# A hybrid decoder layer on one core: the last mixer tile gets its own order, output weights are split one tile sooner, the first output projection stands in its waits

## What is computed

```python
hn = rms_norm(x, norm_mix_g[l])
proj = hn @ w_in[l]
att = swa_sink_attention(q_a, k_a, v_a, ...)
qk_m = causal_conv_silu(jnp.concatenate([q_m, k_m], axis=-1), conv_w[l], conv_b[l])
h_m = mlstm_chunkwise(...)          # state C, n, m carried from chunk to chunk
h_m = rms_norm(h_m, ...).reshape(B, S, ML_WIDTH) * jax.nn.sigmoid(o_m)
x = x + jnp.concatenate([att, h_m], axis=-1) @ w_out[l]
x = x + hier_moe(rms_norm(x, norm_ffn_g[l]), ...)
```

## Time and profile before

| | us |
|---|---|
| median of 3 runs | 953.25 (952.66 to 955.26) |
| the profiled execution, its own time | 951.49 |
| its span from first to last instruction | 949.7 |
| TensorE busy | 875.6 (92%) |
| TensorE weight loads | 704.1 (74%) |
| VectorE busy | 617.7 (65%) |
| ScalarE busy | 563.7 (59%) |
| GpSimd busy | 250.1 (26%) |
| mean granted TensorE clock | 0.956 |

### The profile page before, as it was taken

How to read it: one execution, slowest core, us unless ns; L and a number is a source line. 1 busy time by engine, 2 the same in 40 slices (tenths; PEclk the granted TensorE clock), 3 DMA queues, 4 the chain that set the end, 5 groups by cost and what they waited for, 6 DMA issues and landing times.

```text
span 949.7 us, 18047 instructions
## 1 busy us (share of the span) xinstructions
PE 875.6 (92%) x5337; PEld 704.1 (74%) x5338; DVE 617.7 (65%) x1262; ACT 563.7 (59%) x1003; POOL 250.1 (26%) x395
## 2 busy tenths in 40 slices
PE   6799999999999976799993699999999999999994
PEld 4688888898988865578882567776768688777873
DVE  3766666656666658243467767665569699876992
ACT  3474755637374656022224368865769799787991
POOL 4101011010101100000005035544344444554442
PEclk9989999999999995899996699999999999999998
DMA  9800010101000050343447477975879799888973
GB/s 330 238 24 23 24 45 0 44 0 44 22 22 22 1 200 23 111 153 137 153 162 287 164 259 270 325 273 125 311 254 382 261 380 394 301 302 298 389 274 67
DMA packets 57646, 168.41 MB, mean 177 GB/s; under 512 B 12584, under 2 KB 14928, under 8 KB 57616
## 3 DMA queue, kind: packets, MB, share of 16 engines
q1 hardware_dynamic: 50384, 143.13, 40.6%
q0 software_dynamic: 7232, 24.92, 10.1%
HBM read 143.49 MB, written 24.54 MB: 177 GB/s over the span
## 4 chain that ended last, share of the span: by engine, by line
PE 44%; issue 27%; POOL 13%; DVE 5%; POOLq 5%; DMA 4%; ACT 2%; SPq 0%; ACTq 0%; DVEq 0%
PE bank_j L995 8%; PE bank_j L997 7%; PE bank_j L996 7%; PE bank_j L1089 5%; POOL tick L595 5%; PE bank_j L1100 3%; PE bank_o L1080 3%; POOL hn L629 2%; POOLq L640 2%; PE bank_t L989 2%; POOL out_dram L634 2%; DMA PT<-in_w_in_dram 2%; PE bank_t L1073 2%; POOL row_s L641 1%; PE bank_s L1065 1%
## 5 line engine op out<-in xcount | busy, mean ns | idle before, releaser
L995 PE MATMUL bank_j<-w_high,rows_high 128*128 128x512 f32 x512 | 208.2, 407 | 7.4 <-DVE w_low L1557 5.0
L997 PE MATMUL bank_j<-w_high,rows_low 128*128 128x512 f32 x512 | 202.6, 396 | 0.0
L996 PE MATMUL bank_j<-w_low,rows_high 128*128 128x512 f32 x512 | 202.2, 395 | 0.0
L595 POOL TENSOR_TENSOR tick<-mhalf 1x1 f32<-1x1 f32 x176 | 89.4, 514 | 200.4 <-DVE lg L1931 72.0
L995 PEld LDWEIGHTS bank_j<-w_high,rows_high 128*128 128x128 f32 x512 | 97.7, 191 | 39.4 <-issue 12.7
L1816 DVE TENSOR_TENSOR w_low<-w_res,w_high 128x1024 fp32r<-128x1024 f32 x96 | 114.2, 1218 | 7.0 <-ACT w_high L693 7.0
L997 PEld LDWEIGHTS bank_j<-w_high,rows_low 128*128 128x128 f32 x512 | 97.6, 191 | 21.2
L996 PEld LDWEIGHTS bank_j<-w_low,rows_high 128*128 128x128 f32 x512 | 98.0, 191 | 18.7
L693 ACT ACTIVATE w_high<-w_res 128x1024 fp32r<-128x1024 f32 x96 | 97.6, 1050 | 0.9 <-PE bank_j L997 0.9
L989 PE MATMUL bank_t<-ident,hn 128*128 128x128 f32 x336 | 46.4, 284 | 16.5 <-DVE hn L1587 8.5
L1089 PE MATMUL bank_j<-hnT,w_res 128*128 128x128 f32 x512 | 60.3, 277 | 0.0
(11 more groups left out here) (364 smaller groups left out, 1820.1 us busy)
## 6 DMA issues: line engine op xcount, KB each, us to landing
w_res<-in_w_gate_dram SPq DMA_DIRECT2D x48, 512.0 KB, 7.8
w_res<-in_w_up_dram SPq DMA_DIRECT2D x48, 512.0 KB, 7.2
bias<-in_w_down_dram SPq DMA_DIRECT2D x32, 512.0 KB, 7.9
slot_b<-in_w_gate_dram SPq DMA_DIRECT2D x16, 512.0 KB, 10.2
PT<-in_w_up_dram SPq DMA_DIRECT2D x16, 512.0 KB, 11.2
gmix<-in_w_down_dram SPq DMA_DIRECT2D x16, 512.0 KB, 6.7
h<-in_w_down_dram SPq DMA_DIRECT2D x16, 512.0 KB, 8.3
hn<-in_x_dram SPq DMA_DIRECT2D x8, 512.0 KB, 3.3
```

Of the source, the lines that this page charges most:

```text
L595: pool.tensor_tensor(tick[:, len(ticks):len(ticks) + 1], mhalf[0:1, 0:1], mhalf[0:1, 0:1], ALU.mult)
L995: pe.matmul(out_, ah, bh, start=start, stop=False)
L996: pe.matmul(out_, ah, bl, start=False, stop=False)
L997: return pe.matmul(out_, al, bh, start=False, stop=stop)
```

## The change

- **Output weights sooner.** In tile 6 SyncE loads tile 0's mixed rows and piece 0 of `w_out` (now into `gmix`) as soon as the buffers are free, and pieces 1 to 6 into `wres` right after the last convolution (`pe_cin`). ScalarE copies pieces 0 to 5 and VectorE subtracts 0 to 3 in tile 6; the rest is done in the last tile.
- **The last tile has a function of its own on each engine,** `last_tile` on ScalarE and VectorE, a block in `body` on TensorE. The logits come before the gates' sums, the first exponentials before the gates' exponentials, the gate rows after the first transposed probabilities.
- **The first output projection** goes by pieces (`first_out`): each piece's rows are multiplied into both banks before the next piece. Pieces 0 to 2 stand after the first scores, 3 after the second, 4 after the first values, 5 to 7 at the end.
- **The second tile's mixed rows** are loaded at the start of the last tile, transposed and split at its end; both first x tiles are loaded after the second logits.
- **Dropped:** update of the state, of the running maximum and of the weighted keys in the last tile.
- Code that both kinds of tile use is moved word for word into named functions (`keys_and_gates`, `gate_sums`, `decay_args`, `state_rows` and so on); the diff leaves these out.

```diff
-        slot_out = [*pieces_of(wres, 6), gmix[:, :], wres[:, 0:PW]]
+        slot_out = [gmix[:, :], *pieces_of(wres, 6), gmix[:, :]]
...
-                if main and not nxt:
+                if main and nxt and not ahead:
                     sp.wait_ge(pe_hnT, TILES)
                     load_mix(0)
 
+                    sp.wait_ge(dve_hn, TILES)
+                    load_out(0)
                     sp.wait_ge(pe_cin, TILES)
-                    sp.wait_ge(dve_hn, TILES)
-                    for i in range(OUTP):
-                        if i == OUTP - 1:
-                            sp.wait_ge(lo0, PIECES + 1)
+                    for i in range(1, OUTP - 1):
                         load_out(i)
+                    sp.wait_ge(lo0, PIECES + 1)
+                    load_out(OUTP - 1)
+                if main and not nxt:
+                    load_mix(1)
+                    sp.wait_ge(dve_L1, TILES)
+                    for i in range(2):
+                        sp.dma_start(xin[:, i, :], x2[i * P:(i + 1) * P, :]).then_inc(LDX[i], 16)
+                    sp.wait_ge(lo0, PIECES + OUTP)
+                    sp.dma_start(gffn[:, :], norm_ffn_g[0, :].partition_broadcast(P)).then_inc(ld_gf, 16)
...
-            sp.wait_ge(dve_L1, TILES)
-            sp.dma_start(xin[:, 0, :], x2[0:P, :]).then_inc(LDX[0], 16)
-            sp.wait_ge(lo0, PIECES + OUTP)
-            sp.dma_start(gffn[:, :], norm_ffn_g[0, :].partition_broadcast(P)).then_inc(ld_gf, 16)
...
-                act.wait_ge(pe_om, TILES)
+                act.wait_ge(pe_q if i < FC else pe_vm, TILES)
...
+            def last_tile(t, u):
+
+                act.wait_ge(pe_qkT, t + 1)
+                act.wait_ge(pe_s1, t)
+                cp(qT[:, :, :].rearrange("p a b -> p (a b)"), S0[:, :]).then_inc(act_qT, 1)
+                mix_high(0, 0)
+                act.wait_ge(act_kvg, t + 1)
+                act.wait_ge(pe_o, t)
+                cp(vw[:, u, :], kvg[:, KVW:2 * KVW]).then_inc(act_v, 1)
+                log_gates(t)
+                act.activation(warm[:, 0:1], warm[:, 1:2], ACT.Exp)
+                exps(t, 0, dve_nm0, act_p0)
+                gate_exps(t)
+                pT_copy(t, pe_pT0, act_pT0)
+                for i in range(6, OUTP):
+                    out_high(i)
+                exps(t, 1, dve_nm1, act_p1)
+                decay_exps(t)
+                pT_copy(t, pe_pT1, act_pT1)
+                mix_high(1, 1)
+                state_squares(t, t + 1)
...
+                    if into_last:
+                        out_high(0)
...
                     cp(cin[:, :, TAPS - 1:], J0[:, :].rearrange("p (a b) -> p a b", a=CC)).then_inc(act_cin, 1)
+                    if into_last:
+                        out_high(1)
...
+                    state_squares(t, t + 2)
+                if into_last:
+                    for i in range(2, 4):
+                        out_high(i)
                 if nxt:
                     act.wait_ge(pe_vm, t + 2)
                     wait(act, pe_u, t + 1)
                     cp(vm[:, :, 0:DV], J1[:, :].rearrange("p (a b) -> p a b", a=MH)).then_inc(act_vm, 1)
+                if into_last:
+                    for i in range(4, 6):
+                        out_high(i)
                 if ahead and main:
...
+            def first_out(ks):
+
+                for k in ks:
+                    pe.wait_ge(lo0, PIECES + k + 1)
+                    for half, b in enumerate((J0, J1)):
+                        if k == 0:
+                            pe.wait_ge((act_om, act_vm)[half], TILES)
+                            pe.wait_ge(dve_mixT, 2)
+                        cols = slice(half * HALF, (half + 1) * HALF)
+                        ins = three(b[:, :], MX[0][0][:, k, :], MX[0][1][:, k, :], wo_h[:, k, cols], wo_l[:, k, cols],
+                                    k == 0, k == KC - 1)
+                        if k == KC - 1:
+                            ins.then_inc((pe_y0, pe_y1)[half], 1)
...
+                if main and not nxt:
+                    pe.wait_ge(act_qT, t + 1)
+                    pe.wait_ge(dve_kg, t + 1)
+                    scores(0, pe_s0)
+                    k_rows()
+                    first_out(range(0, 3))
+                    pe.wait_ge(dve_L0, t + 1)
+                    scores(1, pe_s1)
+                    first_out([3])
+                    pe.wait_ge(act_p0, t + 1)
+                    probs_T(pe_pT0)
+                    pe.wait_ge(act_pT0, t + 1)
+                    pe.wait_ge(dve_pT0, t + 1)
+                    gate_rows()
+                    pe.wait_ge(act_v, t + 1)
+                    pe.wait_ge(dve_att, t)
+                    values(0, pe_pv0)
+                    first_out([4])
+                    pe.wait_ge(dve_darg, t + 1)
+                    pe.wait_ge(dve_qg, t + 1)
+                    pe.wait_ge(act_p1, t + 1)
+                    probs_T(pe_pT1)
+                    state_scores()
+                    pe.wait_ge(act_pT1, t + 1)
+                    pe.wait_ge(dve_pT1, t + 1)
+                    values(1, pe_o)
+                    state_values()
+                    mix_T(1)
+                    first_out(range(5, OUTP))
+                    return
...
-            pe.wait_ge(dve_mix, TILES)
-            pe.wait_ge(dve_C, TILES)
+            pe.wait_ge(dve_gT, TILES)
...
+            def last_tile(t, u):
+
+                keys_and_gates(t, u)
+                mix_low(0, 0)
+                dve.wait_ge(pe_pT1, t)
+                logits(t, 0, pe_s0, dve_L0, dve_nm0)
+                gate_sums(t)
+                out_low(4)
+                pT_copy(t, pe_pT0, dve_pT0)
+                logits(t, 1, pe_s1, dve_L1, dve_nm1)
+                decay_args(t)
+                out_low(5)
+                pT_copy(t, pe_pT1, dve_pT1)
+                state_weights(t)
+                for i in range(6, OUTP):
+                    out_low(i)
+                attention(t)
+                state_scales(t)
+                add_first_half(0, 0)
+                mix_low(1, 1)
+                state_rows(t)
...
+                    if into_last:
+                        out_low(0)
...
+                if into_last:
+                    for i in range(1, 4):
+                        out_low(i)
...
+                if first:
+                    dve.wait_ge(ld_gf, 16)
+                    chain(dve.tensor_scalar(gffn[:, :], gffn[:, :], float(D) ** 0.5, None, ALU.mult))
+                    dve.wait_ge(st_mix, 16 * TILES)
```

More of the change, by code:

```diff
@@ L488, in body2 @@
             def body2(t, u, first, last):
-                if not last:
+                if not first and not last:
                     load_mix(t + 1)
@@ L738, in body @@
             def body(t, u, main, nxt, ahead):
                 v = 1 - u
+                if main and not nxt:
+                    last_tile(t, u)
+                    return
+                into_last = main and not ahead
                 if ahead and not main and not nxt:
@@ L762, in body @@
                     cp(vw[:, u, :], kvg[:, KVW:2 * KVW]).then_inc(act_v, 1)
-                    act.wait_ge(dve_az, t + 1)
-                    chain(act.activation(gfz[32:32 + MH, 1, :], gfz[32:32 + MH, 0, :], ACT.Exp, scale=-1.0))
-                    act.activation(gfz[32:32 + MH, 1, :], gfz[32:32 + MH, 1, :], ACT.Ln, bias=1.0).then_inc(act_ln, 1)
-                    if not nxt:
-                        for i in range(4):
-                            out_high(i)
+                    log_gates(t)
                 if nxt:
@@ L1022, in project_out @@
                     pe.wait_ge(dve_mixT, 2 * t + 2)
[L1023 to L1026 removed]
+                pe.wait_ge(read, t)
                 cols = slice(half * HALF, (half + 1) * HALF)
@@ new lines, in state_rows @@
+            def state_rows(t):
+                dve.wait_ge(pool_rhm, t + 1)
+                dve.wait_ge(act_om, t + 1)
+                chain(dve.tensor_tensor(hrr[:, :], hden[:, :], hrs[:, :], ALU.mult))
+                for h in range(MH):
+                    c = h // 2
+                    ins = dve.scalar_tensor_tensor(
+                        mix[:, AW + h * DV:AW + (h + 1) * DV], (S0, S1)[h % 2][:, c * VE:c * VE + DV],
+                        hrr[:, h:h + 1], osg[:, h * DV:(h + 1) * DV], ALU.mult, ALU.mult)
+                ins.then_inc(dve_mix, 1)
@@ L1590, in body @@
             def body(t, u, main, nxt, ahead):
-                v = 1 - u
+                if main and not nxt:
+                    last_tile(t, u)
+                    return
+                into_last = main and not ahead
                 if ahead and not main and not nxt:
```

317 lines of the change are left out of this document (156 added, 161 removed).

## The result

The changed kernel takes **928.73 us** (median of 4 runs, 927.86 to 929.11) beside 952.95 us (952.15 to 955.26) for the kernel before: a ratio of 0.9746, 95% interval 0.9731 to 0.9761. The profiled execution took 928.41 us, its span is 926.6. The forecast was 929.1.

A forecast was written before the change was run, and what follows sets the result against it. TensorE's last-tile waits (8.9 us gate rows, 6.5 us DMA) and half-speed matmuls behind them bound it. 34.1 work + 6.7 waits + 1.5 clock = 42.3 against 66.5 us: 953.25 - 24.2 = 929.1 us, range 926 to 936.

The forecast's parts named there:

- The work: TensorE's matmuls from the last tile's first transposes to the second tile's projection: 34.1 us at full clock.
- (1): TensorE's wait before the last tile's first scores, with VectorE late after piece 1's landing and three subtractions: 2.3 us.
- Rival A: Pieces hold ScalarE's queue longer; piece 1 lands in 6.3 to 9.7 us: 930.9 to 934.3 us, chance 0.14.
- (2): TensorE's wait for the low part of the first tile's rows, made after the late sigmoid: 0.2 us.
- (3): Gate rows in the last tile wait for copies of the first transposed probabilities: 1.0 us.
- (4): TensorE's wait for the second probabilities in the last tile: 0.7 us, bounds 0 and 1.7.
- (5): TensorE's wait for copies of the second probabilities in the last tile: 0.2 us.
- (6): Second tile's projection waits for J0's first half to be read and the rows' low part: 1.5 us.
- (7): Transposes of the first tile's normalised rows wait for VectorE, late after sums, low part and scaling: 0.8 us.
- rival C: Output projections: first tile's scaling waits for the last mix store, third tile's rows may be late; 932.6 us, chance 0.09.
- The clock: Granted clock falls once, early in the last tile after 2.3 us idle: 1.5 us, bounds 0 and twice that.
- Rival D: Clock stays low for the whole stretch, work taking twice as long: 3.6 us slower, 956.9 us, chance 0.02.

The follow-up runs named there:

- three profiles at the full clock: Changed kernel with piece 3 behind the first transposed probabilities (924.29 us), with VectorE's low part before the sum (927.11 us), and with both plus squares before piece 1's copy (922.60 us).
- all pieces at the end: Changed kernel with all eight pieces of the first output projection at the end of the last tile, loads and splits still early: 939.63 us.
- piece 4 sooner: Changed kernel with piece 4 of the first output projection ahead of the gate rows, piece 3 unmoved: 932.00 us, run again unchanged 931.25 us.
- with piece 5 in its place: Changed kernel with piece 4 ahead of the gate rows and piece 5 behind the first values, where piece 4 stood: 930.08 us.

## Why the prediction was right, and where it was not

**Right:** the place, the two waits that go, and the sum. The stretch from the first transposes of the last tile to the second half of the second tile's projection was forecast at 42.3 us and is 42.55 (347.73 to 390.28). Its terms are 34.1 work, 6.7 waits and 1.5 clock against 34.8 work (what the three profiles at the full clock have), 4.4 idle and 3.4 clock. So the sum is right in part by luck: 2.3 us too many waits cancel 0.7 us of work and 1.9 us of clock too few.

**The work, 0.7 us too little.** The prediction halved what ran at 0.50. The rows show less than a factor of two: sixteen values 3.67 us (all pieces at the end) against 1.97, and with all pieces at the end 22.9 us of work that take about 12.5 at the full clock (45.2 busy, 34.8 at the full clock). By that factor of 1.8 the 16.64 us of the earlier trace rows would be 9.1 and not 8.3 us, an estimate that covers the 0.7.

**The waits, 2.3 us too many.** By the numbers of the prediction: (1) the first scores 1.3 instead of 2.3 us. The failed term is the lateness of the tile's end. The landing of piece 1, taken at 4.5 us from the earlier trace rows, took 3.9, and the chain to the squares was 1.2 us longer, not 2.0, in a tile that ran 0.3 us ahead; VectorE came to the last tile's keys at 349.68 us, not at 351.0, and the 4.34 us that it had stood idle there before took up its three subtractions. Rival A, a landing of 6.3 us or more, is refuted. The estimate of 3.2 us by the Trainium skill (DMA: Bandwidth & Descriptors, Anatomy of one DMA), a figure for GpSimd's path, is about as far below the 3.9 as the 4.5 lie above. (2) doesn't show. (3) 0.8 for 1.0. (4) zero for 0.7: piece 4 covers it; with piece 4 moved ahead, 0.6 and 1.4 us were waited there. (5) 0.2 as forecast. (6) 1.4 for 1.5; its cause, the first sum ahead of the low part, is confirmed by the swap of the two. (7) 0.5 for 0.8, and by another cause: by its work alone VectorE would have been in time, but it stood idle 1.68 us for the store of the mixed rows, which is rival C.

**The clock, 1.9 us too little and in the wrong place.** The step that failed is that it falls "once, early, with 2.3 us of idle time". In the profile it did not fall there but within the first values, behind the gate rows, where the prediction had put a sign that it was wrong (a low clock over the gate rows and values); in another execution of the same kernel it fell at both places (9.9 us of work at the low clock, 4.4 us of cost, 39.2 us busy against 34.8). The cost measured with this TensorE program is 0 to 4.4 us, and the bounds given, 0 to 3, were too narrow. What the prediction hadn't seen is that the level can fall among small matmuls even where TensorE is 80% busy or more; that it can stay low among them stood in the earlier trace rows (16.64 of 19.5 us busy at 0.50).

**Rival D** said the clock might stay low for the whole stretch. With all pieces at the end it stayed low for 27.1 us and cost 10.4 (45.2 us busy against 34.8). Its mechanism is real, its price of twice the time a little high (1.8 times), and in the changed order the longest low stretch of two profiles was 6.7 us. That the dense pieces are what ends it is likely from the three orders, but not shown: with piece 4 sooner it once came back without them.

**Rival C** had the right mechanism: VectorE's scaling does wait for the store of the mixed rows,

```profile
385.37 2.04 DVE L1942 SCALAR_TENSOR_TENSOR h<-bias,rsh,gmix 128x1024 f32<-128x1024 f32 x1 [1.68 <-DMA mix_rows<-h]
```

but the store landed 2.7 us after its issue, not 4.5, and on TensorE only 0.45 us is left of it, its wait (7). The third tile's rows weren't late.

**After the stretch.** From there to the first expert's first projection the kernel before takes 121.1 us (414.5 to 535.6), the changed one 122.5 (390.3 to 512.7), with the same waits (5.0, 4.2, 4.2 and 2.4 us in both). Most of the 1.4 us lies in the rank matmuls of the routing. Before and after:

```profile
523.48 1.39 PE L1237 MATMUL bank_j<-cin,hn 128*128 128x260 f32 x4
524.71 0.60 PE L1237 MATMUL bank_j<-q_sb,hn 128*128 128x260 f32 x2
```

```profile
499.58 1.94 PE L1318 MATMUL bank_j<-cin,hn 128*128 128x260 f32 x4
501.32 1.07 PE L1318 MATMUL bank_j<-q_sb,hn 128*128 128x260 f32 x2
```

Six matmuls of the same form take 1.0 us longer at the low clock, again behind a wait that both kernels have. So of 23.9 us won in the stretch 23.1 arrive at the end of the span.

## What to carry to other kernels

Where a stage has no next tile to fill its gaps, bring the next stage's dense matmuls in, and have their operands loaded and split one tile sooner; without any one of the three parts of this the kernel was 9 to 11 us slower. Spread the dense blocks among the groups of small matmuls rather than all at one end, and measure more than one place for each: here one piece moved by one place made the median about 4 us faster or 3 us slower while the sum of waits changed by half a microsecond or less. Price a low clock by the work in it, not by the idle time ahead of it, and give it a range, since two executions of one program fell at different places.

## What the runs showed of the hardware

- The granted clock falls to 0.50 not only behind long gaps: it did so behind 0.83 us of idle time with gate rows of 4 partitions and 64-column values following (changed kernel, 363.0 us), and behind none at all since 350.8 us, again within these values (piece 4 sooner at 365.7 us, and with piece 5 in its place near 366 us). It stayed there while TensorE was busy 22.87 of 27.1 us with small matmuls (all pieces at the end) and 13.08 of 13.7 us (piece 4 sooner).
- It isn't fixed by the program. The same TensorE instructions behind the same 0.83 us wait took 3.61 us in one execution and 2.00 in another; the same first pieces ran at 1.00 in one and from 351.4 to 354.6 us at 0.52 in another. Single executions of one kernel spread by 1 to 7 us, the slower ones mostly at a lower mean clock; not all of that is this stretch, since behind it the changed kernel's two profiles took 536.3 and 537.5 us. What draws the fall stays open.
- At the low level the same matmuls took somewhat less than twice as long: 3.67 us (all pieces at the end, piece 4 sooner) against 1.97 (changed kernel) for the second sixteen values.
- A 512 KB load of `w_out`, the first of six, landed after 3.9 us here, where the three in the earlier trace rows took 4.5 to 9.7 us.
